# Full-bank matmuls in the stages that add to x: high weights times both operand halves at once, both halves added by VectorE

## The reference, cut to what matters

```
first block, layer 0:  h = modulate(rmsnorm(x));  z = h @ w_in  (va, vg, ga, xb, gb, 1024 columns each)
                       ya = silu(layernorm(conv31(va * sigmoid(vg)))) * silu(ga)
                       yb = rglru(xb) * silu(gb)
                       x  = x + gate * (concat(ya, yb) @ ev_w_out)            # 2048 -> 1024
first block, layer 1:  u, g = split(modulate(rmsnorm(x)) @ od_w_in)           # 2048 columns each
                       y = (grouped matmul of multiscale_pool(u)) * scale * silu(g)
                       x = x + gate * (y @ od_w_out);  x = rmsnorm(x)          # 2048 -> 1024
second block:          mixer: f, i, q, u, v, o, ga, gb = h @ w_in;  chunked linear recurrence and gated MLP
                       x = x + gate * (merged @ w_o)                           # 1024 -> 1024
                       a, b = split(modulate(rmsnorm(x)) @ w_up);  x = x + gate * ((silu(a) * b) @ w_down)   # 2816 -> 1024
                       return rmsnorm(x)
```

## Time and profile before

| what | us |
|---|---|
| median of 3 runs (lowest, highest) | 906.91 (905.55, 907.85) |
| span of the profiled execution | 903.1 |
| TensorE busy | 884.7 (98%) |
| VectorE busy | 710.0 (79%) |
| ScalarE busy | 504.7 (56%) |
| GpSimd busy | 142.2 (16%) |
| weight stream and modulation rows, mean | 216 GB/s |

### The profile page before, as it was taken

How to read it: one execution, slowest core, us unless ns; L and a number is a source line. 1 busy time by engine, 2 the same in 40 slices (tenths; PEclk the granted TensorE clock), 3 DMA queues, 4 the chain that set the end, 5 groups by cost and what they waited for, 6 DMA issues and landing times.

```text
span 903.1 us, 17404 instructions
## 1 busy us (share of the span) xinstructions
PE 884.7 (98%) x7132; PEld 829.2 (92%) x7132; DVE 710.0 (79%) x1033; ACT 504.7 (56%) x727; POOL 142.2 (16%) x254
## 2 busy tenths in 40 slices
PE   8999999999999999999999999999999999999996
PEld 6688776689999999989999999999999999999995
DVE  5689667989888999968569975797987998765543
ACT  5474888997845455225554465483535644444441
POOL 0003864710021001300211100300001000000000
PEclk9999999999999999999999999999999999999998
DMA  9946987885776677866638844555556567666661
GB/s 365 388 144 216 306 271 222 280 274 181 214 276 210 230 262 269 293 215 201 184 103 292 303 128 142 178 173 187 155 180 181 172 204 255 187 185 183 196 204 52
DMA packets 55295, 195.45 MB, mean 216 GB/s; under 512 B 7856, under 2 KB 7984, under 8 KB 53808
## 3 DMA queue, kind: packets, MB, share of 16 engines
q1 hardware_dynamic: 39600, 147.73, 50.4%
q0 software_dynamic: 15616, 46.61, 15.2%
HBM read 188.60 MB, written 1.05 MB: 210 GB/s over the span
## 4 chain that ended last, share of the span: by engine, by line
PE 75%; DVE 14%; ACT 4%; issue 3%; DMA 2%; POOL 1%; DVEq 0%; SPq 0%; ACTq 0%; POOLq 0%
PE ps L582 22%; PE ps L584 21%; PE ps L583 21%; DVE w_lo L1415 4%; PE ps L756 3%; PE ps L685 2%; PE px L674 2%; ACT w_hi L980 1%; DVE win L1429 1%; DVE dump L1788 1%; DMA x<-in_xT 1%; DMA raw<-in_stream 1%; DVE li L1429 1%; PE px L861 1%; DVE li L1614 1%
## 5 line engine op out<-in xcount | busy, mean ns | idle before, releaser
L1415 DVE TENSOR_TENSOR w_lo<-raw,w_hi 128x1024 fp32r<-128x1024 f32 x232 | 280.5, 1226 | 83.9 <-ACT w_hi L980 83.3
L980 ACT ACTIVATE w_hi<-raw 128x1024 fp32r<-128x1024 f32 x232 | 242.7, 1055 | 110.8 <-DMA raw<-in_stream 110.0
L582 PE MATMUL ps<-h_hi,w_hi 128*128 128x256 f32 (+1 forms) x864 | 256.0, 296 | 6.2 <-DVE w_lo L1415 2.8
L583 PE MATMUL ps<-h_lo,w_hi 128*128 128x256 f32 (+1 forms) x864 | 251.4, 291 | 0.0
L584 PE MATMUL ps<-h_hi,w_lo 128*128 128x256 f32 (+1 forms) x864 | 251.3, 291 | 0.0
L582 PEld LDWEIGHTS ps<-h_hi,w_hi 128*128 128x128 f32 x864 | 165.3, 191 | 16.6 <-issue 5.7
L583 PEld LDWEIGHTS ps<-h_lo,w_hi 128*128 128x128 f32 x864 | 165.4, 191 | 3.5 <-issue 1.2
L584 PEld LDWEIGHTS ps<-h_hi,w_lo 128*128 128x128 f32 x864 | 165.4, 191 | 2.7
L459 POOL DMA_DIRECT2D modw<-in_mod_w x80 | 42.8, 536 | 391.6 <-DVE modw L1449 250.1
L582 PE MATMUL ps<-h2o_hi,w_hi 128*128 128x256 f32 x352 | 101.5, 288 | 0.0
L584 PE MATMUL ps<-h2o_hi,w_lo 128*128 128x256 f32 x352 | 99.6, 283 | 0.0
(11 more groups left out here) (353 smaller groups left out, 1856.6 us busy)
## 6 DMA issues: line engine op xcount, KB each, us to landing
raw<-in_stream SPq DMA_DIRECT2D x252, 512.0 KB, 3.8
modw<-in_mod_w POOLq DMA_DIRECT2D x80, 512.0 KB, 5.7
m<-in_mod_w SPq DMA_DIRECT2D x8, 1024.0 KB, 19.5
shifts<-upad POOLq DMA_DIRECT2D x128, 35.5 KB, 4.7
c_row<-in_c_rows SPq DMA_DIRECT2D x3, 512.0 KB, 7.6
ctxT<-in_ctxT SPq DMA_DIRECT2D x1, 1024.0 KB, 4.9
x<-in_xT SPq DMA_DIRECT2D x1, 1024.0 KB, 7.1
ctx2T<-in_ctx2T SPq DMA_DIRECT2D x1, 1024.0 KB, 6.5
```

Source lines behind the costliest of these rows:

```text
L582: pe.matmul(o, wh, hi, start=start, stop=False)
L583: pe.matmul(o, wh, lo, start=False, stop=False)
L980: act.activation(w_hi[split[0] % HI_RING][:], raw[n % RING][:], ACT.Copy).then_inc(w_hi_ready, 1)
L1415: v.tensor_tensor(w_lo[n % RING][:], raw[n % RING][:], w_hi[split[0] % HI_RING][:].bitcast(F32), ALU.subtract).then_inc(w_lo_ready, 1)
```

## The change

Per step `k`, the two matmuls that share `w_hi` become one of 512 columns: its moving operand is the pair of halves (hi, lo), its output the whole bank. The product with `lo` thus lands in columns 256 to 511, and the product of `w_lo` with `hi` goes to columns 0 to 255 as before. VectorE then adds both halves of the bank to x, in two instructions, the second waiting for the first; only the second frees the bank. The last tile of each stage (t = 7) and wo's first keep the three matmuls and the single add. To give one access pattern to both halves, each pair is now one allocation: ya and yb keep their places, as do ff's halves; y_lo moves to just behind y_hi, m_lo to just behind m_hi.

```diff
+        y_both = at("y_both", W + 78, [2, 16, T], F32R)
+        y_hi, y_lo = y_both[:, 0], y_both[:, 1]
-        y_lo = at("y_lo", W + 97.25, [16, T], F32R)
...
-        m_hi, m_lo = at("m_hi", W + 60, [KT, T], F32R), at("m_lo", W + 88, [KT, T], F32R)
+        m_both = at("m_both", W + 60, [2, KT, T], F32R)
+        m_hi, m_lo = m_both[:, 0], m_both[:, 1]
...
+            def full_bank(name, t, both, ready=None, tiles=KT, first=True, last=True):
+
+                wh, wl = split_weights(name, t)
+                o = bank_of(name, t) if first else psum_of(name, t)
+                for k in range(tiles):
+                    if ready is not None:
+                        pe.wait_ge(ready[0], ready[1] + k + 1)
+                    hi_lo = both(k)
+                    if first and k == 0:
+                        pe.matmul(o[:, :], wh[:, k, :], hi_lo, start=True, stop=False)
+                        mm = pe.matmul(o[:, 0:T], wl[:, k, :], hi_lo[:, 0], start=False, stop=False)
+                    else:
+                        pe.matmul(o[:, 0:T], wl[:, k, :], hi_lo[:, 0], start=False, stop=False)
+                        mm = pe.matmul(o[:, :], wh[:, k, :], hi_lo, start=False, stop=last and k == tiles - 1)
+                mm.then_inc(tile_done, 1)
...
+            def yb_tile(t, ready=None):
+                if t < KT - 1:
+                    full_bank("yb", t, lambda k: yb_both[:, :, k, :], ready, first=False)
+                else:
+                    thirds("yb", t, *yb, first=False)
...
-            for t in range(1, KT):
-                thirds("wo", t, lambda k: m_hi[:, k, :], lambda k: m_lo[:, k, :])
+            for t in range(1, KT - 1):
+                full_bank("wo", t, lambda k: m_both[:, :, k, :])
+            thirds("wo", KT - 1, lambda k: m_hi[:, k, :], lambda k: m_lo[:, k, :])
...
                 xt = x[:, t, :]
+                if t < KT - 1 and (name, t) != ("wo", 0):
+                    S.do(v.scalar_tensor_tensor(out=xt, in0=psum_of(name, t)[:, T:2 * T], scalar=gate[:, t:t + 1],
+                                                in1=xt, op0=ALU.mult, op1=ALU.add))
+                    S.sync()
                 v.scalar_tensor_tensor(out=xt, in0=psum_of(name, t)[:, 0:T], scalar=gate[:, t:t + 1],
                                        in1=xt, op0=ALU.mult, op1=ALU.add).then_inc(free_of(name, t), 1)
```

More of the change, by code:

```diff
@@ L209, in build @@
         ga = at("ga", W, [KT, T])
-        ya_hi = at("ya_hi", W, [KT, T], F32R)
+        ya_both = at("ya_both", W, [7, KT, T], F32R)[:, 0::6]
+        ya_hi, ya_lo = ya_both[:, 0], ya_both[:, 1]
         conv = at("conv", W + 8, [KT, T])
@@ L219, in build @@
         gb = at("gb", W + 16, [KT, T])
-        yb_hi = at("yb_hi", W + 24, [KT, T], F32R)
-        yb_lo = at("yb_lo", W + 40, [KT, T], F32R)
-        ya_lo = at("ya_lo", W + 48, [KT, T], F32R)
+        yb_both = at("yb_both", W + 24, [3, KT, T], F32R)[:, 0::2]
+        yb_hi, yb_lo = yb_both[:, 0], yb_both[:, 1]
         LB = 4
@@ L240, in build @@
         win = [at("win0", W + 68, [16, PW]), at("win1", W + 73, [16, PW])]
-        y_hi = at("y_hi", W + 78, [16, T], F32R)
+        y_both = at("y_both", W + 78, [2, 16, T], F32R)
+        y_hi, y_lo = y_both[:, 0], y_both[:, 1]
         vr1 = at("vr1", W + 94, [T])
@@ L292, in build @@
         h3_hi, h3_lo = at("h3_hi", W + 16, [KT, T], F32R), at("h3_lo", W + 24, [KT, T], F32R)
-        ff_hi, ff_lo = at("ff_hi", W + 32, [FT, T], F32R), at("ff_lo", W + 54, [FT, T], F32R)
+        ff_both = at("ff_both", W + 32, [2, FT, T], F32R)
+        ff_hi, ff_lo = ff_both[:, 0], ff_both[:, 1]
         v4 = at("v4", W + 76, [2, T])
@@ L729, in _, with ya_tile @@
             yb = (lambda k: yb_hi[:, k, :], lambda k: yb_lo[:, k, :])
+            def ya_tile(t, ready=None):
+                if t < KT - 1:
+                    full_bank("ya", t, lambda k: ya_both[:, :, k, :], ready, last=False)
+                else:
+                    thirds("ya", t, *ya, last=False)
+            def yb_tile(t, ready=None):
+                if t < KT - 1:
+                    full_bank("yb", t, lambda k: yb_both[:, :, k, :], ready, first=False)
+                else:
+                    thirds("yb", t, *yb, first=False)
             for t in range(4):
-                thirds("ya", t, *ya, last=False, ready=(ya_ready, 0) if t == 0 else None)
+                ya_tile(t, (ya_ready, 0) if t == 0 else None)
             for t in range(4):
-                thirds("yb", t, *yb, first=False, ready=(yb_ready, 0) if t == 0 else None)
+                yb_tile(t, (yb_ready, 0) if t == 0 else None)
             for t in range(4, KT):
-                thirds("ya", t, *ya, last=False)
+                ya_tile(t)
             for t in range(4, KT):
-                thirds("yb", t, *yb, first=False)
+                yb_tile(t)
             keep_busy(4)
@@ L758, in _, with out_tile @@
                 mm.then_inc(tile_done, 1)
+            def out_tile(name, t, ready):
+                k0, first = (0, True) if name == "oa" else (KT, False)
+                if t < KT - 1:
+                    full_bank(name, t, lambda k: y_both[:, :, k0 + k, :], ready, first=first, last=not first)
+                else:
+                    thirds(name, t, lambda k: y_hi[:, k0 + k, :], lambda k: y_lo[:, k0 + k, :], first=first,
+                           last=not first)
             for t0_ in range(0, KT, 4):
                 for t in range(t0_, t0_ + 4):
-                    thirds("oa", t, lambda k: y_hi[:, k, :], lambda k: y_lo[:, k, :], last=False,
-                           ready=(y_ready, 0) if t == 0 else None)
+                    out_tile("oa", t, (y_ready, 0) if t == 0 else None)
                 for t in range(t0_, t0_ + 4):
-                    thirds("ob", t, lambda k: y_hi[:, KT + k, :], lambda k: y_lo[:, KT + k, :], first=False,
-                           ready=(y_ready, KT) if t == 0 else None)
+                    out_tile("ob", t, (y_ready, KT) if t == 0 else None)
             both = ((h2o_hi, h2o_lo), (h2c_hi, h2c_lo))
@@ L960, in _ @@
                 for n, name in enumerate(("d0", "d1", "d2")):
-                    thirds(name, t, lambda k: ff_hi[:, n * KT + k, :], lambda k: ff_lo[:, n * KT + k, :],
-                           tiles=min(KT, FT - n * KT), first=(n == 0), last=(n == 2),
-                           ready=(ff_ready, n * KT) if t == 0 else None)
+                    ready = (ff_ready, n * KT) if t == 0 else None
+                    if t < KT - 1:
+                        full_bank(name, t, lambda k: ff_both[:, :, n * KT + k, :], ready, min(KT, FT - n * KT), n == 0, n == 2)
+                    else:
+                        thirds(name, t, lambda k: ff_hi[:, n * KT + k, :], lambda k: ff_lo[:, n * KT + k, :],
+                               tiles=min(KT, FT - n * KT), first=(n == 0), last=(n == 2))
             two_chunks(px[0], sq5, 8, 6 * KT)
```

## The result

The changed kernel takes 912.32 us (median of 13 runs, 909.44 to 917.34) against 906.98 for the kernel before in the same comparison: a ratio of 1.0059, 95% interval 1.004 to 1.0077, or 3.6 to 7.0 us slower. Forecast were 910.5 and slower; the range held the time, the forecast's own range (909.3 to 911.8) did not.

The account below looks back on a forecast made before the run. It took VectorE-ScalarE rings to bound the ev_w_out and od_w_out ends, VectorE wo, TensorE down. Terms 3.4 + 2.2 + 0.1 - 2.05 = +3.6 us on 906.91 gave 910.5 us, range 904 to 913.5.

Parts of the forecast that it names:

- the forecast's own range: Whole kernel: 909.3 us if a second add costs 0.41 us, 911.8 if 0.57; forecast chance 0.45.
- The ring in od_w_out: od_w_out: VectorE's add, ScalarE's squares and rounding, VectorE's subtract wait in a circle; second adds lengthen it, +3.4 us.
- The ring in ev_w_out: ev_w_out: same circle of VectorE and ScalarE waits with one square; five second adds count, +2.2 us.
- wo, +0.1: wo stage: it turns VectorE-bound at 3.01 us a turn and TensorE's 0.6 us is spent waiting, +0.1 us.
- Down, -2.05: Down stage: TensorE sets the end and the extra adds have room, so the matmul gain counts, -2.05 us.
- 13.3 ns a pair: TensorE: two 256-column matmuls take 240 ns, one of 512 takes 227; the gain where TensorE sets the pace.
- Rival 4: Full-bank matmuls mixed with 256-column ones gain nothing: rings as forecast, down 0, 912.6 us; chance 0.05.
- 2.5 ns a pair: TensorE: the skill's gap at full clock taken as the gain; down 0.4 us, sum ending at 912.2; set aside.
- rival 1: Gap after od_w_out: TensorE's clock falls from 2.4 to 1.2 GHz, 2 us more, 912.5 us; chance 0.24.
- The sum: Whole kernel: 3.4 + 2.2 + 0.1 - 2.05 = +3.6 us, giving 910.5 us.
- Rivals 2 and 3: 2: added work hides in VectorE's idle time, 901.2, chance 0.10. 3: rings catch up, only down gains, 904.9, chance 0.16.

Follow-up runs that it names:

- e4: The changed kernel with eight matmuls on ones, for no result, put in front of the statistics after od_w_out: 911.25 us, ratio 1.0057.
- e1: The changed kernel with the second add taken out, so the high-weight, low-activation product is missing from x: 903.19 us, ratio 0.9969.
- e2: The kernel before with a first add of zero times the product in the same 27 tiles, matmuls unchanged: 912.25 us, ratio 1.0059.
- e3: The changed kernel with adds behind the low weights of tile t + 3, not t + 4, in ev_w_out, od_w_out and down: 907.09 us, ratio 1.0021.
- e7: The changed kernel with ev_w_out as in the kernel before and, in od_w_out alone, adds behind low weights of tile t + 3: 903.64 us, ratio 0.9969.
- e6: The changed kernel with the matmuls of two contraction steps put together, low, low, high, high: 910.57 us, ratio 1.006.
- e8: The kernel before with only od_w_out's adds moved, behind the low weights of tile t + 3 in place of t + 4: 905.68 us, ratio 0.9991.

## Why the prediction was right, and where it was wrong

- *The ring in od_w_out, +3.4*: right. +3.36 by the adds, and 63.20 - 59.85 = +3.35 on TensorE's path with the clock held (e4 against before). e1 and e2 show that it is the adds; e3 and e7 that it is their place.
- *The ring in ev_w_out, +2.2*: right, 2.41 by the reciprocal and 0.53 + 1.89 = 2.42 on TensorE.
- *wo, +0.1*: about nothing, as said; -0.28 + 0.10 in the trace, which lies within what that stretch varies by. VectorE sets the pace, as forecast: its adds stand 2.94 us apart (704.58 to 707.52) without idle time, against 3.01 forecast.
- *Down, -2.05*: the mechanism was right, the size wrong. The mis-sized term is the 13.3 ns a pair: 63.24 - 62.16 = 1.08 us over 154 steps are 7.0 ns. The 0.2267 us of the earlier trace rows come from an unmixed run of 512 columns, and in down low and high matmuls in turn do not reach the sum of their unmixed prices. In od_w_out they come closer: e7 gains 46.15 - 45.00 = 1.15 us over 112 steps, 10.3 ns each, and ten steps of the changed kernel were at the forecast's price. What decides between the prices is open. Rival 4 named the mixing and put the gain at nothing; in down the truth lay halfway. The Trainium skill (TensorE: Matmul & The Clock Gate, section Back-to-back issue gap) gives the columns divided by 2.4, plus 2.5 ns, as the gap of an isolated matmul, and says that a stream with weight loads goes by other prices. Taken as a price all the same, it would have made 2.5 ns a pair; the measured 7.0 ns, and 11.7 in e6's order (1.80 us over 154), lie above that.
- *The clock, rival 1 at 0.24*: this is the step that failed. The argument against it, that no pause of the kernel before its end has it, said nothing of a pause that only the change makes, one pair of matmuls in 3.6 us, and the forecast had itself worked out its length. It cost 1.61 us (after against e4) where 2 were priced; a matmul at the lower level took 0.21 us for 0.12, somewhat under twice as long. The Trainium skill (same page, section HAM oscillation) speaks of this loss between bursts of matmuls, there with waits for DMA, and the traces of after, e2 and e6 agree: 0.50 granted after the gap.
- *The sum*: +3.65 forecast; 2.42 + 3.35 + 1.61 - 0.28 + 0.10 - 1.08 = +6.12 in the trace, +5.3 between the medians. The clock and the halved gain in down, 1.61 and 0.97, are the difference of 2.5 but for 0.1. The range held because it took in rival 1. That 912.32 lies so near rival 1's 912.5 is partly luck, for its sum still has the full gain in down. Rival 4 (912.6) and the price of 2.5 ns a pair (912.2) come as near without being right: down gained 1.08 where they have 0 and 0.4, and neither has the clock.
- *Rivals 2 and 3* fall: the 1.89 us of idle time hid nothing (a turn of 4.04 us for 3.52), and the tiles without an add did not catch up (the reciprocal 2.41 us late, the last add of od_w_out 3.36).

## What to carry to other kernels

An idle time inside a ring is not slack: before costing an added instruction at nothing, follow the wait round, and if it comes back to the instruction itself, move the work out of the ring (here, one weight tile earlier) rather than shorten it. Where a change makes a new pause of TensorE, here 3.6 us with one pair of matmuls, do not argue the clock away because the old pauses left it alone: give it a term in the sum. Price a mix of matmul widths from a mixed run of the same stage, and try more than one order.

## What the runs showed of the hardware that was not expected

- The same 256- and 512-column matmuls in turn take 0.353 us a step over the down stage and 0.347 over ten steps of od_w_out. In down two by two is 4.7 ns a step cheaper, and all low then all high (61.61 us for the stage) no better than that (61.44); in od_w_out neither gains more than 0.06 us (44.94 for 45.00). Why is open.
- In the gap with one pair of matmuls in 3.6 us the granted clock still read 1.00; it fell only as work came back (473 to 474: 0.68, then 0.50), and was at 1.00 again from 477 on.
- The multiplies on two modulation rows of the first stage, which wait for the rows' arrival, start at 97.3 to 97.6 and 98.6 to 101.3 us in six of the twelve traces (before, e2, e4, e6, e7, e8) and at 100.5 to 101.9 and 103.4 to 105.6 in the others; the first changed tile begins at 234.9 to 236.4 in the former and at 240.8 to 243.5 in the latter. What decides it was not tried. Part of the delay is the clock again: in all six late traces TensorE stands still for 3.1 to 5.3 us there and the granted clock then falls to 0.50, in none of the other six. In after the next 48 matmuls take 7.23 us from first to last start for 5.74 in before. The matmul behind the wait, and a window of after:

```profile
106.73 0.39 PE L584 MATMUL ps<-h_hi,w_hi 128*128 128x256 f32 x1 [3.48 <-DVE w_lo L1455]
```

```profile
109.00:110.00 1.00, 1.00 (x7) 1.00 (x6) 1.00 (x2) 1.00 (x2) 1.00 (x3) 0.50 0.95 281
```
